# Weight stage: one-hot products two batches at a time between half score blocks, and the first-index one-hots built by a 16-bit comparison and a multiplication

## What is computed

```python
cand = (v1[..., :, None] + v2[..., None, :]).reshape(...)
best, c = lax.top_k(cand, PK_TOPK)                      # 8 heads x 16 = 128 choices a token
e1 = jnp.take_along_axis(i1, c // PK_TOPK, axis=-1)     # first index, 0 to 127
e2 = jnp.take_along_axis(i2, c % PK_TOPK, axis=-1)      # second index, 0 to 127
expert = e1 * N_KEYS + e2
gate = jax.nn.softmax(best, axis=-1)
...
act = jax.nn.gelu(jnp.einsum('tkd,td->tk', u_sel, xt), approximate=False)
return jnp.einsum('tk,tkd->td', gt * act, v_sel)
```

## Time and profile before

| what | value |
|---|---|
| median of 3 runs | 1673.12 us (1671.1 to 1674.15) |
| profiled execution | 1673.59 us, its span 1671.8 us |
| granted PE clock over the span | 0.998 of full |
| PE busy | 1661.5 us (99%) |
| DVE busy | 1437.0 us (86%) |
| ACT busy | 724.1 us (43%) |
| POOL busy | 757.7 us (45%) |
| chain that ended last | PE 97% |

### The profile page before, as it was taken

The page is one execution under the profiler, slowest core; times in us unless marked ns, Lnnn a source line. Parts: engine busy times, 40 slices in busy tenths (PEclk is TensorE's granted clock), DMA queues, the critical chain, the costliest instruction groups (busy, mean ns, idle before and its releaser), DMA issues.

```text
span 1671.8 us, 33592 instructions
## 1 busy us (share of the span) xinstructions
PE 1661.5 (99%) x12009; PEld 1435.8 (86%) x12009; DVE 1437.0 (86%) x2759; ACT 724.1 (43%) x1053; POOL 757.7 (45%) x605
## 2 busy tenths in 40 slices
PE   9999999999999999999999999999999999999998
PEld 6878788788888999999998888888888888888886
DVE  5379988666598999999997999999999999999996
ACT  5565445453422333467774434343333333333333
POOL 0000000010054477688885665655555565555550
PEclk9999999999999999999999999999999999999999
DMA  5221122244322355578889999999999999999993
GB/s 188 79 74 53 47 90 78 84 176 149 116 81 85 131 184 175 185 223 255 253 261 367 410 410 410 410 410 410 409 394 394 385 385 383 387 384 401 393 350 112
DMA packets 166339, 424.98 MB, mean 254 GB/s; under 512 B 14160, under 2 KB 75728, under 8 KB 166000
## 3 DMA queue, kind: packets, MB, share of 16 engines
q1 hardware_dynamic: 117328, 244.52, 41.0%
q0 software_dynamic: 48928, 179.33, 27.8%
HBM read 382.87 MB, written 39.45 MB: 253 GB/s over the span
## 4 chain that ended last, share of the span: by engine, by line
PE 97%; ACT 1%; DVE 1%; issue 0%; DVEq 0%; ACTq 0%
PE unit L453 97%; DVE oneh L2220 0%; PE unit L608 0%; ACT L1241 0%; PE unit L1030 0%; ACT ld L1241 0%; ACT aa L1241 0%; ACT k L1241 0%; ACT best L1241 0%; ACT pk L1241 0%; DVE wL L1720 0%; ACT sqj L1241 0%; ACT wst L1241 0%; ACT kn L1241 0%; ACT uH L1241 0%
## 5 line engine op out<-in xcount | busy, mean ns | idle before, releaser
L453 PE MATMUL unit<-h2H,uH 128*128 128x352 f32 x1024 | 334.7, 328 | 0.2 <-ACTq L1572 0.2
L453 PE MATMUL unit<-h2L,uH 128*128 128x352 f32 x1024 | 328.8, 323 | 0.0
L2440 POOL DMA_INDIRECT ring<-u_tab,idx x128 | 172.6, 1348 | 156.1 <-DVE accs L2307 122.3
L453 PE MATMUL unit<-vL,aH 128*128 128x512 f32 (+1 forms) x768 | 241.7, 396 | 0.0
L453 PE MATMUL unit<-vH,aH 128*128 128x512 f32 (+1 forms) x768 | 239.4, 392 | 0.0
L453 PE MATMUL unit<-vH,aL 128*128 128x512 f32 (+1 forms) x768 | 238.9, 392 | 0.0
L2440 POOL DMA_INDIRECT ring<-v_tab,idx x128 | 172.6, 1348 | 139.1 <-DVE ring L2292 132.6
L453 PEld LDWEIGHTS unit<-h2H,uH 128*128 128x128 f32 x1024 | 192.8, 188 | 4.6 <-issue 0.4
L453 PEld LDWEIGHTS unit<-h2L,uH 128*128 128x128 f32 x1024 | 193.0, 188 | 2.8
L453 PE MATMUL unit<-h2H,uL 128*128 128x352 f32 x1024 | 191.2, 325 | 0.0
L1241 ACT ACTIVATE vH<-vraw 128x1024 fp32r<-128x1024 f32 x128 | 135.0, 1055 | 91.0 <-PE unit L453 91.0
(11 more groups left out here) (331 smaller groups left out, 3309.1 us busy)
## 6 DMA issues: line engine op xcount, KB each, us to landing
uraw<-uT SPq DMA_DIRECT2D x128, 512.0 KB, 6.4
vraw<-v_tab SPq DMA_DIRECT2D x128, 512.0 KB, 7.6
wraw<-wall SPq DMA_DIRECT2D x68, 512.0 KB, 3.3
w_dram<-wst SPq DMA_DIRECT2D x11, 1920.0 KB, 8.6
wg<-w_dram SPq DMA_DIRECT2D x30, 704.0 KB, 7.0
g_dram<-ge SPq DMA_DIRECT2D x64, 176.0 KB, 1.9
gl<-g_dram SPq DMA_DIRECT2D x32, 352.0 KB, 9.0
gate_dram<-gst POOLq DMA_DIRECT2D x16, 256.0 KB, 2.3
```

Source lines behind the costliest of these rows:

```text
L453: return pe.matmul(out, lhsT, rhs, start=start, stop=stop, skip_group_check=True)
L2440: pool.indirect_dma_start(out=ring[k][:, :], out_offset=None, in_=(u_tab, v_tab)[half], in_offset=bass.IndirectOffsetOnAxis(ap=rows[:, m:m ...
```

## The change

On PE, two batches (8 products, 16 MATMUL instructions) now follow each other directly, and then two quarters of the score block (12 matmuls). On DVE the four TENSOR_SCALARs of a batch give way to a TENSOR_TENSOR comparison of a 16-bit iota with the 16-bit first index, over all four tokens at once (512 elements per partition, token innermost), and a TENSOR_TENSOR multiplication with the f32 gate, which reads the 16-bit result with a step of four elements and writes `rh` in f32. Between the two stands the unchanged `oh2` comparison. There are two buffers of the 16-bit result, and a semaphore `hot_ready` from the comparison to the multiplication. The transposed first index is copied from PSUM as 16-bit, and a 16-bit iota of 512 elements is made once before the candidates are picked.

```diff
+    iota4 = at("iota4", 82, [P, NK, 4], U16)
+    hot1 = at("hot1", 84, [P, 2, NK, 4], U16)
+    first = at("first", 88, [P, TD], U16)
...
             def beside_w(i, j):
-                for b in range(4):
-                    batch = 16 * i + 4 * j + b
-                    pe.wait_ge(oh2_ready, batch + 1)
-                    pe.wait_ge(rh_ready, batch + 1)
-                    pe.wait_ge(wst_ready, batch + 1)
-                    o = bank[6 + b % 2]
-                    for k in range(4):
-                        last = mm(o[:, k * P:(k + 1) * P], oh2[:, b, k, :], rh[:, b, k, :])
-                    last.then_inc(wmm_done, 1)
-                    scores(PRE_T + 4 * i + j, j % 2, b)
+                for pair in range(2):
+                    for b in (2 * pair, 2 * pair + 1):
+                        batch = 16 * i + 4 * j + b
+                        pe.wait_ge(oh2_ready, batch + 1)
+                        pe.wait_ge(rh_ready, batch + 1)
+                        pe.wait_ge(wst_ready, batch + 1)
+                        o = bank[6 + b % 2]
+                        for k in range(4):
+                            last = mm(o[:, k * P:(k + 1) * P], oh2[:, b, k, :], rh[:, b, k, :])
+                        last.then_inc(wmm_done, 1)
+                    for quarter in (2 * pair, 2 * pair + 1):
+                        scores(PRE_T + 4 * i + j, j % 2, quarter)
...
+            tick(dve.tensor_copy(iota4[:, :, :], bc(C(C_IOTA), 4)))
...
-            dve.tensor_copy(et[:, 0, :], ps("e1T")[:, 0:TD]).then_inc(take_sem("e1T"), 1)
+            dve.tensor_copy(first[:, :], ps("e1T")[:, 0:TD]).then_inc(take_sem("e1T"), 1)
...
                     dve.wait_ge(wmm_done, 16 * i + 4 * j + b + 1)
-                    for k in range(4):
-                        tok = bass.ds(2 * T_W * i + 16 * j + 4 * b + k, 1)
-                        tsc(rh[:, b, k, :], C(C_IOTA), et[:, 0, tok], et[:, 2, tok], ALU.is_equal, ALU.mult)
+                    batch = 16 * i + 4 * j + b
+                    toks = bass.ds(2 * T_W * i + 16 * j + 4 * b, 4)
+                    tt(hot1[:, b % 2, :, :], iota4[:, :, :], first[:, toks].unsqueeze(1).broadcast_to([P, NK, 4]),
+                       ALU.is_equal).then_inc(hot_ready, 1)
                     two = bass.ds(2 * T_W * i + 16 * j + 4 * b + POOL_HOT, 4 - POOL_HOT)
                     tt(oh2[:, b, POOL_HOT:, :], C(C_IOTA).unsqueeze(1).broadcast_to([P, 4 - POOL_HOT, NK]),
-                       et[:, 1, two].unsqueeze(2).broadcast_to([P, 4 - POOL_HOT, NK]), ALU.is_equal).then_inc(rh_ready, 1)
+                       et[:, 1, two].unsqueeze(2).broadcast_to([P, 4 - POOL_HOT, NK]), ALU.is_equal)
+                    dve.wait_ge(hot_ready, batch + 1)
+                    tt(rh[:, b, :, :], hot1[:, b % 2, :, :].rearrange("p e t -> p t e"),
+                       et[:, 2, toks].unsqueeze(2).broadcast_to([P, 4, NK]), ALU.mult).then_inc(rh_ready, 1)
```

More of the change, by code:

```diff
@@ L371, in build @@
         rh_ready, wmm_done, wst_ready = sem("rh_ready"), sem("wmm_done"), sem("wst_ready")
+        hot_ready = sem("hot_ready")
         wg_copied = [sem(f"wg{i}_copied") for i in range(2)]
```

## The result

The changed kernel takes 1706.91 us (median of 5 runs, 1706.58 to 1707.69) against 1673.12; the ratio is 1.0199, 95% interval [1.0188, 1.0211]. The profiled execution's span is 1704.9 us, 33.1 more than before. 32.2 of these are in the weight stage: from the start of the first product to that of `begin_sum` in PE's timeline it was 882.59 - 719.12 = 163.47 us and is now 915.79 - 720.16 = 195.63. The stretch ahead of it is 1.04 us longer, all that follows 0.1 shorter.

What follows compares the result with a forecast made beforehand. The prediction took PE to bound the weight stage. PE -0.2 us, DVE, POOL and iota 0 gave 1673.4 us for an execution like the profiled one, 1672.9 for the median, stated as 1673; range 1671 to 1700 us.

Steps and rivals of the forecast that it cites:

- rival (b): Weight stage: POOL becomes the bound, one-hots averaging 0.99 us cost 23 us, or 0.92 costs 10 us (1683); chance 0.10.
- What bounded the kernel before: Weight stage: PE busy for all 163.08 us, with no time left over for alternating between batches and scores.
- PE's new order: Weight stage: removing 44 of 88 alternations, each worth 0, and a 0.22 us end wait gains 0.2 us, at most 0.6.
- DVE's costs: DVE's weight stage: comparison 0.34 us start to start, multiplication 0.61 to 1.07, batch 1.29 to 1.75; lower value taken.
- rival (a): DVE's weight stage: multiplication reads its stepped operand slowly, DVE becomes the bound, 16 to 39 us, near 1700; chance 0.28.
- (c): DVE's weight stage: the 16-bit comparison is not doubled in speed, step 7.88 us, 10 us lost, 1683; chance 0.04.
- The step that failed: POOL in the weight stage: two one-hots in 1.5 us, mean 0.81 us, under the 0.86 at which POOL binds.
- The range: Whole kernel time: 1671 us, below the forecast by run-to-run spread, to 1700 us, the middle of DVE becoming the bound.
- The iota: Candidate stretch: at most another 0.69 us DVE operation, hidden where DVE later waits 1.37 us for ACT.
- The shared way to memory: Weight stage: a POOL one-hot costs DVE up to 0.13 us; DVE's step becomes 6.3 to 7.3 us, under 7.41.

Runs made afterwards that it cites:

- run 1: The kernel before with only PE's new order (two batches, then two quarters): 1673.09 us, ratio 0.9999.
- 2: The changed kernel with PE's old order (one batch, one quarter), DVE's part kept: 1703.55 us, ratio 1.0179 to the kernel before.
- 3: The changed kernel with POOL building one of four oh2 one-hots per batch and DVE three: 1674.75 us, ratio 1.0005 to the kernel before.
- 4: The changed kernel with all four oh2 one-hots on DVE and none on POOL: 1674.62 us, ratio 1.0008 to the kernel before.
- run 5: The changed kernel with DVE waiting for each one-hot operation's completion before the next, none added behind `uL`: 1717.14 us, ratio 1.0264 to the kernel before.
- run 6: The changed kernel with one more DVE wait, the multiplication waiting for the oh2 comparison's completion: 1683.97 us, ratio 1.0062 to the kernel before.
- 7: The changed kernel with one more DVE wait, the next batch's 16-bit comparison waiting for the multiplication's completion: 1692.75 us, ratio 1.0116 to the kernel before.
- run 8: The changed kernel with DVE's two oh2 one-hots as one-input TENSOR_SCALARs, one behind the other: 1704.42 us, ratio 1.0189 to the kernel before.
- run 9: The changed kernel with one-input oh2 one-hots interleaved: comparison, one-hot, multiplication, one-hot. 1679.71 us, ratio 1.0026 to the kernel before.
- 10: The changed kernel ordered comparison, one-hot, multiplication, one-hot, with the oh2 one-hots as two-input TENSOR_TENSORs of 128 elements: 1702.65 us, ratio 1.0150 to the kernel before.
- run 11: The kernel before with the 16-bit iota copy alone, made and not used: 1675.14 us, ratio 1.0007.

## Why the prediction was wrong

The forecast of no change failed, and the time, 1706.91, lies above the range that ended at 1700. It was rival (b), POOL becomes the bound, which had a chance of 0.10. The term that failed is POOL's: two turns per DVE batch, a mean of 0.81 us, where the trace has one turn per round and 1.07.

- **What bounded the kernel before, PE's new order:** right. Alternations worth 0 (run 1: 0.9999), pairs 1.75 us, no PE wait at the end. The gain of 0.2 us is too small for the runs to show.
- **DVE's costs:** right, at the low ends: comparison 0.41 undisturbed, multiplication 0.68, and a read with a step of 8 bytes costs nothing here. With it rival (a), at 0.28, falls, and so does (c). The Trainium skill, "Vector Engine (DVE) Microarchitecture Reference", section 5.2, gives 1.73 ns per element for one source that hops 4 KiB at every element; this step of 8 bytes did not cost that (678 ns for 512 elements). The Trainium skill, "SBUF — State Buffer", section "Door 1: The DMA port swizzle", asks for two hits per 16-byte line, and the trace agrees. This was the point that I had weighed most, and the wrong one.
- **The step that failed:** "it gets its turn at the end of the multiplication, its next request comes 0.55 us later, while `oh2` runs (16-bit comparison 0.34 + 0.1, then `oh2` to 0.78), so the cycle is 0.78; the next turn is at the end of the multiplication, 0.71 later." I let POOL in at every change between two DVE operations. In the trace it is passed over at the first one when DVE's next two-input operation is already lined up (83 of 86), and gets in at the second: a round is three operations (1.37 us), one one-hot and not two. The mean of 0.81 became 1.07 and passed the 0.86 from which POOL binds. With that bound (1.074 - 0.86) x 176 = 38 us, against 32 measured in the stage, so it was about right. Nothing in the earlier trace rows could show it, since before no DVE operation with two inputs was followed by another, except once a step (`uL` behind `oh2`); I took a rule for rows of a kind that the trace did not have.
- **Rival (b)'s price:** 10 us, at most 23, was too low for the same reason. Its form, a mean of 0.99, lets one one-hot in two wait for the whole multiplication; it lacks the meetings with `uL`, 1.68 us for each of the 18 that were passed over there.
- **The range:** its upper end came from (a) alone. One turn per round for (b) could have been worked out beforehand: 1.37 + 0.60 = 1.97 us for the two one-hots of a batch, and 1.66 for one of the eight of a step, is a mean of (4 x 0.60 + 3 x 1.37 + 1.66) / 8 = 1.02, an estimate of 28 us and 1701. So the end at 1700 was too low, and even this estimate falls 6 us short.
- **The iota:** expected hidden by 1.37 us of waiting. That wait went in every kernel with the copy. The cost stays between 0 and 2.7 us.
- **The shared way to memory:** one-hots that met two-input operations took 1.39 us and not 0.60. The Trainium skill's rule in "SBUF — State Buffer", section "Who interferes with whom", spoke against the change, and the trace agrees; it says who contends, and the runs add that it is not the time held but the turns that count.

Shown by runs: that DVE's part costs (1, 2), that POOL's number of turns is what binds (3, 4), that what stands behind a two-input operation decides whether POOL gets in (5 to 10). The last can be counted in all traces with POOL one-hots, but run 11's: where a two-input operation was lined up behind the running one, 631 of 639 one-hots were passed over at the change; where a one-input operation was lined up, 3 of 178; where nothing was, none of 373. Not shown: why it is so inside the chip, and why the 8 got in and the 3 did not.

No version beats the kernel before: PE fills the stage without a gap, so the best are equal to it (runs 1, 3 and 4).

## What to carry to other kernels

Before DVE work is recast from one-input into two-input operations beside a busy POOL, count POOL's turns: if DVE's two-input operations follow each other without a wait, allow it one turn per two or three of them (here one per round of three), and compare that with the operations that POOL must do. Faster DVE instructions can be a loss when DVE was not the bound, because it runs ahead and starves the neighbour that is needed as well. The cures are to give POOL fewer operations, or to put a one-input operation or a wait behind each long two-input one. A wait has its price (0.22 to 0.32 us each here); with one behind every operation DVE itself became the bound (run 5).

## What the hardware showed unexpectedly

- An added wait on DVE made the kernel 23 us faster (run 6 against the changed kernel), and a mere change of order 25 us (run 9 against run 8), or 27 by the ratios.
- POOL may be passed over: behind the multiplication it stood through the following comparison as well, 1.39 us for a 0.60 us operation; 83 one-hots were passed over like this. Where nothing was lined up behind the running operation, none was, in any run. When it got in at 777.17 it held DVE up by only 0.09 us.
- A 16-bit read with a step of 8 bytes, with an f32 result, ran as fast as a contiguous f32 one (678 ns for 512 elements, against 693), while the 16-byte step of the earlier trace rows was slower (386 ns for 128).
- PE's clock fell to 0.55 to 0.59 over 4 us behind a stretch in which it was busy for 1.36 of 3 us.
